# RMSNorm statistics of an encoder kernel: one full-precision product replaced by two on a high and a low part

## The chip, the cores and the metric

The kernel runs on one core of a Trainium2 chip. The metric is the time of one execution on the device in microseconds, the median of several runs. PE is the tensor engine, DVE the vector engine, ACT the scalar engine, POOL the GpSimd engine and SP the engine that issues most of the transfers; each runs its own instruction stream in order, and they meet only in semaphores.

## What is computed

A two-layer encoder trunk on 512 tokens of 1024 channels in float32. Layer 0 mixes tokens by 2-D neighbourhood attention, layer 1 by sliding-window attention; each is followed by a squared-ReLU MLP. An RMSNorm stands ahead of each of the four sub-layers and at the end.

```python
def rms_norm(x, g):
    xf = x.astype(jnp.float32)
    y = xf * lax.rsqrt(jnp.mean(xf * xf, axis=-1, keepdims=True) + EPS)
    return (y * g.astype(jnp.float32)).astype(x.dtype)

def reference(x, mix_norm, mlp_norm, final_norm, ...):
    for i in range(DEPTH):                      # DEPTH = 2
        h = rms_norm(x, mix_norm[i])
        if i % 2 == 0:
            x = x + neighbourhood_attention(h, ...)
        else:
            x = x + sliding_window_gqa(h, ...)
        h = rms_norm(x, mlp_norm[i])
        x = x + squared_relu_mlp(h, mlp_w_in[i], mlp_w_out[i])
    return rms_norm(x, final_norm)
```

## The kernel before

**Layout.** `x` is kept transposed in SBUF: channels on the 128 partitions in 8 tiles, k = 0 to 7, and 512 tokens along the free dimension. The weights stream in as 180 chunks of 8 blocks of 128x128, in two alternating buffers `w_raw`.

**Dense products.** Every value that enters a dense product is split into a high part (rounded to a shorter format, F32R, by a copy on ACT) and a low part (the value minus its high part, by DVE), and `product` issues three matmuls for each block: high by high, high by low, low by high (L370 to L372 in turn). A group is 8 such blocks and fills one of the two accumulators `acc`; it uses one chunk of weights. For chunk c ACT makes `w_hi` (L733) and DVE `w_lo` (L999); PE waits for `w_split` before the first block of a chunk and, from the third group on, for `acc_taken`, which says that DVE has read the accumulator.

**The norm.** There are five norms, n = 0 to 4. Norm 0 is at the start, 1 ahead of the first MLP, 2 ahead of the second attention, 3 ahead of the second MLP, and 4, the final one, is built differently (`last_squares`, `last_norm`, `last_statistics`). For each tile k, `prepare_x` on ACT makes `h_hi` (L743) and the square of `x` (L744), and `finish_x` on DVE makes `h_lo` (L1010) and adds the square to `sqsum` (L1016), which raises `h_split`. Ahead of norms 1 and 3 the tiles come from `output_projection`, ahead of norm 2 from the down loop of `mlp`. The dense product runs on the tiles not yet normalised. The scale is put on its result: the statistics product on PE (a matrix of ones by `sqsum`, so that each partition gets the sum over all channels, in full precision, L420), then `deviation` on ACT (square root, L757), `reciprocal_deviation` on DVE (L1021, 3.35 us), and `scale_tile` (L1027), which reads `acc`.

**Order around it.** The order on each engine is written out by hand. On PE, `part_after_norm` runs the first group behind a norm block by block as the tiles come, and puts the statistics ahead of the last block, k = 7. A second group follows; the third needs the third chunk of weights, whose `w_lo` stands on DVE behind the reciprocal and the first scaling. On ACT, `load_sqrt` is a tiny square root (128x1) that makes the table of that function come in ahead of the time it is needed. It stands at the end of `output_projection` and of each MLP half and ahead of the first `deviation`. Copies and squares run under any table; an exponential in attention brings in another one. `SPLIT_AFTER` says behind which tile which chunk is split.

Of the kernel before, what the change touches and what calls it, by code (L numbers as in the profile page):

```python
# [22 lines left out]
P = 128  # L23
# [75 lines left out]
def encoder(nc, xT, wstream, gains, rpb, sinks, rel_table, na_mask, onehot, out):  # L99
# [3 lines left out]
    with ExitStack() as ctx:  # L103
        def sb(name, shape, dt=F32):
            return ctx.enter_context(nc.sbuf_tensor(name, shape, dt))
# [24 lines left out]
        rstd = sb("rstd", [P, SEQ])  # L130
        scaled = sb("scaled", [P, 2, SEQ])
        ident, ones = sb("ident", [P, P]), sb("ones", [P, P])
        mask = sb("mask", [P, QT, WC])
# [37 lines left out]

        x_prepared, h_split, sq_cleared = sem("x_prepared"), sem("h_split"), sem("sq_cleared")
        stat_done, std_made, rstd_made = sem("stat_done"), sem("std_made"), sem("rstd_made")

# [192 lines left out]
        def _(pe):  # L367
# [49 lines left out]
            def statistics(n):  # L417

                pe.wait_ge(h_split, KT * (n + 1))
                nc.tensor.matmul(flat(misc_ps[:]), ones[:], sqsum[:], start=True, stop=True).then_inc(stat_done, 1)  # L420

            def part_after_norm(c, g, n):

                for k in ALL:
                    pe.wait_ge(h_split, KT * n + k + 1)
                    if k == KT - 1:
                        statistics(n)
                    part(c, g, h_tile, [k])

            def transpose_v(blocks):  # L430
# [259 lines left out]

            pe.wait_ge(filled, 1)
            pe.wait_ge(ident_made, 1)
            na_step(At(0), attend=False)
# [33 lines left out]
        def _(act):  # L727
# [23 lines left out]
            def load_sqrt():  # L751

                nc.scalar.activation(one[:, 0:1], ones[:, 0:1], ACT.Sqrt)

            def deviation(n):
# [60 lines left out]
            def na_step(m, dense=True, attend=True, before=True):  # L816
# [9 lines left out]
                if dense and m.a == 0:  # L826
                    load_sqrt()
                    deviation(0)
# [20 lines left out]
            def output_projection(ch, gr, norm):  # L849
                split_weights(At(ch + EARLY))  # L850
                for k in range(KT):
                    prepare_x(norm, At(k), lambda: act.wait_ge(acc_taken, gr + k + 1))
                    if k in SPLIT_AFTER:
                        split_weights(At(ch + SPLIT_AFTER[k]))
                load_sqrt()

            def last_squares():

                act.wait_ge(h_split, KT * NORMS - 2)
                for n, t in enumerate(half_tokens):  # L860
                    act.wait_ge(acc_taken, LAST_G + 1 + n)
                    nc.scalar.activation(last_square[:, t], x[:, KT - 1, t], ACT.Square).then_inc(x_prepared, 1)
                    if n == 0:
                        load_sqrt()
                    act.wait_ge(stat_done, NORMS + n)
                    nc.scalar.activation(rstd[:, t], last_stats[n], ACT.Sqrt, bias=eps[:], scale=1.0 / D
                                         ).then_inc(std_made, 1)

            def mlp(ch, gr, ti, sq, norm):
                for half in range(2):  # L870
# [17 lines left out]
                    def down(n, i):  # L888
# [7 lines left out]
                        if (c + 1).a < CHUNKS:  # L896
                            split_weights(c + 1)

                    with act.Fori(0, KT // 2 - 1) as i:
                        down(0, i)  # L900
                        down(1, i)
# [4 lines left out]
                    down(KT - 1, None)  # L906
                load_sqrt()

# [45 lines left out]
            act.wait_ge(filled, 2)  # L954
            nc.scalar.activation(one[:, 0:1], ones[:, 0:1], ACT.Square)
            split_weights(At(0))
            for k in range(KT):
                prepare_x(0, At(k), lambda: act.wait_ge(x_landed[k], 16))
                if k == 5:
                    split_weights(At(1))  # L960
            na_step(At(0), attend=False)
            na_step(At(1), before=False)
# [33 lines left out]
        def _(dve):  # L996
# [8 lines left out]
            def finish_x(n, k):  # L1005
# [8 lines left out]
                if tile.a >= 1:  # L1014
                    dve.wait_ge(h_split, tile.v)
                nc.vector.tensor_tensor(sqsum[:], sqsum[:], probs[:, SEQ * k.odd:SEQ * (k.odd + 1)],  # L1016
                                        ALU.add).then_inc(h_split, 1)

            def reciprocal_deviation(n):
# [137 lines left out]
            def output_projection(ch, gr, norm):  # L1157
# [8 lines left out]
                for k in range(KT):  # L1166
                    if k < EARLY - 1:
                        add(k + 1)
                    elif k >= EARLY:
                        add(k)  # L1170
                    finish_x(norm, At(k))
                    if k in SPLIT_AFTER:
                        split_weights(At(ch + SPLIT_AFTER[k]))

            def last_norm():
# [30 lines left out]
            def mlp(ch, gr, ti, norm):  # L1206
                for half in range(2):
# [28 lines left out]
                    if norm == 3 and half == 1:  # L1236
                        last_norm()
                        return
                    down(KT - 1, None)

            def sw_logits(p, n):
# [66 lines left out]
            nc.vector.memset(ones[:], 1.0).then_inc(filled, 1)  # L1308
            nc.vector.memset(eps[:], EPS).then_inc(filled, 1)
            clear_squares(0)  # L1310
            split_weights(At(0))
            dve.wait_ge(gain_landed, 16)
            for k in range(KT):
                finish_x(0, At(k))
                if k == 5:
                    split_weights(At(1))
            na_step(At(0), attend=False)
            dve.wait_ge(consts_landed, 16 * 2)
# [139 lines left out]
```

## Time and profile before

| | us |
|---|---|
| median of 3 runs | 1162.21 |
| lowest, highest | 1161.75, 1163.99 |
| the profiled execution, its time | 1161.89 |
| its span | 1160.2 |
| PE busy in it | 1136.2 (98%) |
| DVE, ACT busy | 640.2 (55%), 506.6 (44%) |

The span reaches from the first to the last instruction that the profiler recorded; the execution's time is 1.7 us longer. Times in the rows are microseconds from the start of the span. Matmuls overlap, so the distance from one start to the next says what one costs, and not its duration.

### The profile page before, as it was taken

To read this page: it belongs to the slowest core of one execution; us is meant where nothing else is said; L and a number is where in the kernel's file an instruction comes from. 1 tells how busy PE (TensorE), PEld (TensorE's weight loads), DVE (VectorE), ACT (ScalarE), POOL (GpSimd) and SP (SyncE) were. 2 spreads that over 40 slices of the span, in tenths; PEclk is the share of its full clock that TensorE was granted. 3 is DMA by queue.
4 is the path that set the end of the run, shared out by engine and by line. 5 is a ranking of instruction groups with operands and counts; after the bars stand their busy time and mean duration, and the time that the engine had idled before them with its cause. 6 is when DMAs were issued, how large, how long until landed. Compare 5 with 4: busy or idle time off the path is not lost.

```text
span 1160.2 us, 16677 instructions
## 1 busy us (share of the span) xinstructions
PE 1136.2 (98%) x5610; PEld 933.9 (80%) x5610; DVE 640.2 (55%) x1020; ACT 506.6 (44%) x907; POOL 136.7 (12%) x243
## 2 busy tenths in 40 slices
PE   6999999999999999999999999999999999999996
PEld 4788888878888888888887788787888888888886
DVE  7687888665443234443445787766544223544335
ACT  6677776654341124342233666644433112433221
POOL 4744532230000000000000222100000000000000
PEclk9999999999999999999999999999999999999999
DMA  7322231242322322322322122122332232232222
GB/s 212 108 84 74 68 104 57 82 124 92 107 91 91 108 91 91 108 90 91 108 83 81 57 58 64 51 73 78 103 104 96 90 106 93 90 105 95 90 90 91
DMA packets 36850, 106.73 MB, mean 92 GB/s; under 512 B 8224, under 2 KB 10544, under 8 KB 36816
## 3 DMA queue, kind: packets, MB, share of 16 engines
q1 hardware_dynamic: 31680, 98.98, 26.1%
q0 software_dynamic: 4992, 7.29, 2.8%
q8 instruction: 20, 0.33, 0.1%
q14 instruction: 14, 0.11, 0.0%
q10 hardware_dynamic: 144, 0.02, 0.0%
HBM read 102.92 MB, written 3.34 MB: 92 GB/s over the span
## 4 chain that ended last, share of the span: by engine, by line
PE 91%; DVE 3%; SPq 1%; issue 1%; ACT 1%; POOL 1%; DMA 0%; DVEq 0%; ACTq 0%; POOLq 0%
PE acc L370 27%; PE acc L371 26%; PE acc L372 26%; PE s_ps L442 3%; PE om_ps L476 2%; PE pt_ps L641 2%; PE om_ps L472 1%; PE om_ps L500 1%; PE pt_ps L463 1%; SPq L268 1%; PE om_ps L432 1%; POOL bias_pairs L298 1%; PE s_ps L370 1%; PE s_ps L372 1%; PE s_ps L371 1%
## 5 line engine op out<-in xcount | busy, mean ns | idle before, releaser
L733 ACT CAST w_hi<-w_raw 128x1024 fp32r<-128x1024 f32 x180 | 189.1, 1050 | 405.1 <-PE acc L372 401.3
L370 PE MATMUL acc<-h_hi,w_hi 128*128 128x512 f32 x800 | 324.0, 405 | 10.7 <-DVE sqsum L1016 10.2
L372 PE MATMUL acc<-h_hi,w_lo 128*128 128x512 f32 x800 | 313.2, 391 | 0.0
L371 PE MATMUL acc<-h_lo,w_hi 128*128 128x512 f32 x800 | 313.1, 391 | 0.0
L999 DVE TENSOR_TENSOR w_lo<-w_raw,w_hi 128x1024 fp32r<-128x1024 f32 x180 | 223.2, 1240 | 144.1 <-ACT w_hi L733 143.7
L370 PE MATMUL acc<-u_hi,w_hi 128*128 128x512 f32 (+1 forms) x624 | 241.4, 387 | 0.9 <-DVE w_lo L999 0.9
L372 PE MATMUL acc<-u_hi,w_lo 128*128 128x512 f32 (+1 forms) x624 | 239.5, 384 | 0.0
L371 PE MATMUL acc<-u_lo,w_hi 128*128 128x512 f32 (+1 forms) x624 | 239.4, 384 | 0.0
L370 PEld LDWEIGHTS acc<-h_hi,w_hi 128*128 128x128 f32 x800 | 151.0, 189 | 50.0 <-issue 14.1
L372 PEld LDWEIGHTS acc<-h_hi,w_lo 128*128 128x128 f32 x800 | 151.0, 189 | 32.4
L371 PEld LDWEIGHTS acc<-h_lo,w_hi 128*128 128x128 f32 x800 | 151.5, 189 | 29.0 <-issue 1.2
L1027 DVE SCALAR_TENSOR_TENSOR scaled<-acc,rstd 128x512 f32<-128x512 f32 x90 | 62.0, 688 | 143.3 <-PE acc L372 142.6
L370 PEld LDWEIGHTS acc<-u_hi,w_hi 128*128 128x128 f32 x624 | 117.2, 188 | 26.1 <-DVE w_lo L999 2.3
L372 PEld LDWEIGHTS acc<-u_hi,w_lo 128*128 128x128 f32 x624 | 117.3, 188 | 23.4
L371 PEld LDWEIGHTS acc<-u_lo,w_hi 128*128 128x128 f32 x624 | 117.3, 188 | 22.3
L320 POOL DMA_DIRECT2D bias_pairs<-t_shifted x64 | 32.2, 505 | 463.7 <-ACT esink L925 454.4
L777 ACT ACTIVATE probs<-probs,nmax 128x256 f32<-128x256 f32 (+1 forms) x128 | 67.9, 532 | 38.4 <-DVE nmax L1090 38.4
L1146 DVE TENSOR_TENSOR x_res<-acc,x_res 128x512 f32 (+1 forms) x39 | 26.9, 690 | 101.7 <-PE acc L372 101.7
L1037 DVE TENSOR_TENSOR u_lo<-scaled,u_hi 128x512 f32 (+1 forms) x80 | 58.5, 732 | 12.6 <-ACT u_hi L769 12.2
L310 POOL TENSOR_TENSOR bias_masked<-bias_pairs,mask 128x256 f32<-128x256 f32 x64 | 52.3, 857 | 75.1 <-DVE nmax L1090 73.2
L743 ACT ACTIVATE h_hi<-x_res,gain 128x512 fp32r<-128x512 f32 (+1 forms) x32 | 23.1, 722 | 71.9 <-DVE x_res L1146 62.9
L769 ACT CAST u_hi<-scaled 128x512 f32 (+1 forms) x80 | 49.8, 622 | 9.7 <-DVE scaled L1027 2.5
(107 smaller groups left out, 999.1 us busy)
## 6 DMA issues: line engine op xcount, KB each, us to landing
w_raw<-in_wstream SPq DMA_DIRECT2D x180, 512.0 KB, 3.3
bias_pairs<-rpb_shifted POOLq DMA_DIRECT2D x64, 48.0 KB, 2.9
bias_pairs<-t_shifted POOLq DMA_DIRECT2D x64, 48.0 KB, 2.2
x_res<-in_xT SPq DMA_DIRECT2D x8, 256.0 KB, 4.6
out_y<-x_res SPq DMA_DIRECT2D x16, 128.0 KB, 1.8
t_shifted<-vT POOLq DMA_DIRECT2D x16, 31.0 KB, 2.1
rpb_shifted<-rpb_pad POOLq DMA_DIRECT2D x8, 45.0 KB, 5.1
rpb_shifted<-rpb_pad SPq DMA_DIRECT2D x8, 45.0 KB, 7.6
```

Source lines behind the costliest of these rows:

```text
L310: ins = nc.gpsimd.tensor_tensor(bias_m[:, g, i, :, :].rearrange("p c r -> p r c"), rows[:, :, U0[j]:U0[j] + WC], mask[:, j:j + 1, :].to_br ...
L320: pool.dma_start(bias[QC * a:QC * (a + 1), pair.odd, :, :], t5_dram[:, heads, at:at + BAND]).then_inc(t5_bias_landed[pair.odd], 16)
L370: nc.tensor.matmul(dst, a[0], b[0], start=start, stop=False)
L371: nc.tensor.matmul(dst, a[0], b[1], start=False, stop=False)
L372: return nc.tensor.matmul(dst, a[1], b[0], start=False, stop=stop)
L442: ins = nc.tensor.matmul(dst(hh), a[s, queries[0], queries[1]], b[s, keys[0], keys[1]], start=start, stop=stop)
L733: nc.scalar.copy(w_hi[:, c.odd, :], w_raw[:, c.odd, :]).then_inc(w_hi_made, 1)
L769: nc.scalar.copy(dst, src).then_inc(tile_hi, 1)
L777: return nc.scalar.activation(src, src, ACT.Exp, bias=nmax[:, slot, i:i + 1], scale=-1.0, accum_out=rsum[:, slot, i:i + 1])
L999: nc.vector.tensor_tensor(w_lo[:, c.odd, :], w_raw[:, c.odd, :], f32(w_hi[:, c.odd, :]), ALU.subtract).then_inc(w_split, 1)
L1027: nc.vector.scalar_tensor_tensor(out=dst, in0=order(acc[g.odd][:]), scalar=factor, in1=order(rstd[:]), op0=op, op1=ALU.mult).then_inc(acc_ ...
L1037: nc.vector.tensor_tensor(order[0](dst), order[1](scaled[:, e.odd, :]), order[0](f32(hi)), ALU.subtract).then_inc(tile_split, 1)
```

## The change

The sum of squares is split like every other operand: ACT copies `sqsum` into `sq_hi`, rounded, and DVE subtracts to get `sq_lo`. The statistics of norms 0 to 3 become two products with a rounded matrix of ones (`ones_r`, made once at the start by DVE), and they stand behind block k = 7 of the first group instead of ahead of it. The final norm keeps its full-precision products. `load_sqrt` moves: to the very start in place of a tiny square, behind tile k = 3 (EARLY - 1) in `output_projection`, and ahead of the down loop in the second half of each MLP; the one in `last_squares` goes.

```diff
+        sq_hi, sq_lo = sb("sq_hi", [P, SEQ], F32R), sb("sq_lo", [P, SEQ], F32R)
+        ones_r = sb("ones_r", [P, P], F32R)
@@ PE
             def statistics(n):
 
-                pe.wait_ge(h_split, KT * (n + 1))
-                nc.tensor.matmul(flat(misc_ps[:]), ones[:], sqsum[:], start=True, stop=True).then_inc(stat_done, 1)
+                pe.wait_ge(sq_split, n + 1)
+                nc.tensor.matmul(flat(misc_ps[:]), ones_r[:], sq_hi[:], start=True, stop=False)
+                nc.tensor.matmul(flat(misc_ps[:]), ones_r[:], sq_lo[:], start=False, stop=True).then_inc(stat_done, 1)
 
             def part_after_norm(c, g, n):
 
                 for k in ALL:
                     pe.wait_ge(h_split, KT * n + k + 1)
-                    if k == KT - 1:
-                        statistics(n)
                     part(c, g, h_tile, [k])
+                statistics(n)
@@ ACT
+            def squares_high(n):
+
+                act.wait_ge(h_split, KT * (n + 1))
+                nc.scalar.copy(sq_hi[:], sqsum[:]).then_inc(sq_hi_made, 1)
@@ ACT, na_step
                 if dense and m.a == 0:
-                    load_sqrt()
                     deviation(0)
@@ ACT, output_projection
                     if k in SPLIT_AFTER:
                         split_weights(At(ch + SPLIT_AFTER[k]))
-                load_sqrt()
+                    if k == EARLY - 1:
+                        load_sqrt()
+                squares_high(norm)
@@ ACT, last_squares
-                    if n == 0:
-                        load_sqrt()
@@ ACT, mlp
+                    if half == 1:
+                        load_sqrt()
                     with act.Fori(0, KT // 2 - 1) as i:
                         down(0, i)
                         down(1, i)
...
                     down(KT - 1, None)
-                load_sqrt()
+                squares_high(norm + 1)
@@ ACT, start
-            nc.scalar.activation(one[:, 0:1], ones[:, 0:1], ACT.Square)
+            load_sqrt()
...
+            squares_high(0)
@@ DVE
+            def squares_low(n):
+
+                dve.wait_ge(sq_hi_made, n + 1)
+                nc.vector.tensor_tensor(sq_lo[:], sqsum[:], f32(sq_hi[:]), ALU.subtract).then_inc(sq_split, 1)
@@ DVE, end of output_projection
+                squares_low(norm)
@@ DVE, end of mlp
                     down(KT - 1, None)
+                    if half == 1:
+                        squares_low(norm + 1)
@@ DVE, start
+            dve.wait_ge(filled, 1)
+            nc.vector.tensor_copy(ones_r[:], ones[:]).then_inc(ones_rounded, 1)
...
+            squares_low(0)
```

In the listings that follow, the added lines have shifted the line numbers: the three matmuls of a block are L370 to L372 before and L373 to L375 after.

PE at norm 1, the end of the first group behind the norm (`acc<-h` are its blocks 6 and 7, `om_ps` is the bank that the statistics fill), before:

```order
L370 MATMUL acc<-h_hi,w_hi 128x512
L371 MATMUL acc<-h_lo,w_hi 128x512
L372 MATMUL acc<-h_hi,w_lo 128x512
L420 MATMUL om_ps<-sqsum,ones 128x512
L370 MATMUL acc<-h_hi,w_hi 128x512
L371 MATMUL acc<-h_lo,w_hi 128x512
L372 MATMUL acc<-h_hi,w_lo 128x512
```

And with the change:

```order
L373 MATMUL acc<-h_hi,w_hi 128x512
L374 MATMUL acc<-h_lo,w_hi 128x512
L375 MATMUL acc<-h_hi,w_lo 128x512
L373 MATMUL acc<-h_hi,w_hi 128x512
L374 MATMUL acc<-h_lo,w_hi 128x512
L375 MATMUL acc<-h_hi,w_lo 128x512
L423 MATMUL om_ps<-sq_hi,ones_r 128x512
L424 MATMUL om_ps<-sq_lo,ones_r 128x512
```

The statistics moved behind the three matmuls of block 7 and are two.

DVE at norm 1, from the last tile to the reciprocal, before:

```order
L1146 TENSOR_TENSOR x_res<-acc,x_res 128x512
L1010 SCALAR_TENSOR_TENSOR h_lo<-x_res,gain,h_hi 128x512
L1016 TENSOR_TENSOR sqsum<-sqsum,probs 128x512
L999 TENSOR_TENSOR w_lo<-w_raw,w_hi 128x1024
L1021 RECIPROCAL rstd<-rstd 128x512
```

And with the change:

```order
L1162 TENSOR_TENSOR x_res<-acc,x_res 128x512
L1021 SCALAR_TENSOR_TENSOR h_lo<-x_res,gain,h_hi 128x512
L1027 TENSOR_TENSOR sqsum<-sqsum,probs 128x512
L1010 TENSOR_TENSOR w_lo<-w_raw,w_hi 128x1024
L1033 TENSOR_TENSOR sq_lo<-sqsum,sq_hi 128x512
L1037 RECIPROCAL rstd<-rstd 128x512
```

The new subtraction stands behind the split of a weight chunk.

ACT ahead of norm 1, tiles 3 and 4 of `output_projection`, with the change:

```order
L737 CAST w_hi<-w_raw 128x1024
L747 ACTIVATE h_hi<-x_res,gain 128x512
L748 ACTIVATE probs<-x_res 128x512
L757 ACT_TABLE_LOAD
L757 ACTIVATE one<-ones 128x1
L747 ACTIVATE h_hi<-x_res,gain 128x512
L748 ACTIVATE probs<-x_res 128x512
```

The table load now stands between two tiles; before, it stood behind the last split of weights:

```order
L733 CAST w_hi<-w_raw 128x1024
L753 ACT_TABLE_LOAD
L753 ACTIVATE one<-ones 128x1
L757 ACTIVATE rstd<-om_ps,eps 128x512
L733 CAST w_hi<-w_raw 128x1024
```

In its old place comes the copy that makes `sq_hi`.

## Rows read from the trace of the kernel before

**Rows 1.** Page: engine's busy us, share, instructions; ACT's busy tenths in 40 slices.

```profile
PE 1136.2 (98%) x5610; PEld 933.9 (80%) x5610; DVE 640.2 (55%) x1020; ACT 506.6 (44%) x907; POOL 136.7 (12%) x243
...
ACT  6677776654341124342233666644433112433221
```

**Rows 2.** Waits of PE, whole span: us in total, times, longest.

```profile
PE acc L370 <- DVE sqsum L1016: 10.2, 4, 8.2
PE acc L370 <- DVE w_lo L999: 1.4, 4, 0.5
```

**Rows 3.** Timeline, PE, norms 1 and 3: start, duration, instruction, [idle before <-releaser].

```profile
256.80 0.40 PE L372 MATMUL acc<-h_hi,w_lo 128*128 128x512 f32 x1
257.03 1.02 PE L420 MATMUL om_ps<-sqsum,ones 128*128 128x512 f32 x2
...
258.13 0.40 PE L371 MATMUL acc<-h_lo,w_hi 128*128 128x512 f32 x1
...
263.81 0.39 PE L372 MATMUL acc<-h_hi,w_lo 128*128 128x512 f32 x1
...
264.78 0.39 PE L371 MATMUL acc<-h_lo,w_hi 128*128 128x512 f32 x1
...
803.07 1.02 PE L420 MATMUL om_ps<-sqsum,ones 128*128 128x512 f32 x2
```

**Rows 4.** Timeline, ACT, norm 1: the table load and the square root.

```profile
255.40 1.28 ACT L753 ACT_TABLE_LOAD   x1
256.69 0.20 ACT L753 ACTIVATE one<-ones 128x1 f32<-128x1 f32 x1
258.09 0.69 ACT L757 ACTIVATE rstd<-om_ps,eps 128x512 f32<-128x512 f32 x1 [1.20 <-PE om_ps L420]
```

**Rows 5.** Timeline, DVE, norm 1: last addition, splits before and behind the reciprocal.

```profile
255.14 0.69 DVE L1016 TENSOR_TENSOR sqsum<-sqsum,probs 128x512 f32<-128x512 f32 x1
255.74 1.22 DVE L999 TENSOR_TENSOR w_lo<-w_raw,w_hi 128x1024 fp32r<-128x1024 f32 x1
...
263.10 1.22 DVE L999 TENSOR_TENSOR w_lo<-w_raw,w_hi 128x1024 fp32r<-128x1024 f32 x1
```

**Rows 6.** Timeline, DVE and then PE, norm 2.

```profile
605.47 1.22 DVE L999 TENSOR_TENSOR w_lo<-w_raw,w_hi 128x1024 fp32r<-128x1024 f32 x1
...
612.54 1.22 DVE L999 TENSOR_TENSOR w_lo<-w_raw,w_hi 128x1024 fp32r<-128x1024 f32 x1
613.67 0.69 DVE L1037 TENSOR_TENSOR k_lo<-scaled,k_hi 128x512 fp32r<-128x512 f32 x1
...
606.76 1.02 PE L420 MATMUL om_ps<-sqsum,ones 128*128 128x512 f32 x2
...
614.14 0.40 PE L371 MATMUL acc<-h_lo,w_hi 128*128 128x512 f32 x1
```

**Rows 7.** Timeline, ACT around tile 3 ahead of norm 1, and PE behind it.

```profile
236.96 0.62 ACT L744 ACTIVATE probs<-x_res 128x512 f32<-128x512 f32 x1
239.60 0.72 ACT L743 ACTIVATE h_hi<-x_res,gain 128x512 fp32r<-128x512 f32 x1 [2.02 <-DVE x_res L1146]
...
246.69 0.50 PE L370 MATMUL acc<-u_hi,w_hi 128*128 128x512 f32 x1 [0.47 <-DVE w_lo L999]
```

**Rows 8.** Start: timeline of DVE, ACT, PE; windows with busy us by engine, PEclk, DMA.

```profile
17.57 0.68 DVE L1016 TENSOR_TENSOR sqsum<-sqsum,probs 128x512 f32<-128x512 f32 x1
...
19.83 0.69 ACT L757 ACTIVATE rstd<-om_ps,eps 128x512 f32<-128x512 f32 x1 [1.90 <-PE om_ps L420]
...
41.66 0.55 PE L463 MATMUL pt_ps<-ident,probs 128*128 128x128 f32 x3 [1.87 <-ACT probs L812]
...
18.90:22.20 3.30, 3.30 (x9) 2.23 (x8) 1.65 (x1) 1.73 (x2) 0.91 (x2) 0.53 0.71 176
43.00:46.00 3.00, 3.00 (x17) 2.36 (x17) 0.67 (x2) 2.85 (x4) 2.66 (x6) 0.50 0.33 70
```

**Rows 9.** Timeline, ACT, final norm: the first square root.

```profile
1146.23 0.47 ACT L866 ACTIVATE rstd<-om_ps,eps 128x256 f32<-128x256 f32 x1 [1.20 <-PE om_ps L592]
```

More of the change, by code:

```diff
@@ L172, in encoder @@
         x_prepared, h_split, sq_cleared = sem("x_prepared"), sem("h_split"), sem("sq_cleared")
+        ones_rounded, sq_hi_made, sq_split = sem("ones_rounded"), sem("sq_hi_made"), sem("sq_split")
         stat_done, std_made, rstd_made = sem("stat_done"), sem("std_made"), sem("rstd_made")
@@ L691, in _ @@
             pe.wait_ge(filled, 1)
+            pe.wait_ge(ones_rounded, 1)
             pe.wait_ge(ident_made, 1)
```

## The prediction

> **What bounds the kernel now.** I read the page's list of engines first: PE is busy for 98% of the span [rows 1], so a microsecond taken from PE is worth a microsecond only where nothing else ends last. The waits of PE come next, since they show such places [rows 2]. There are few. Most of the first is the start of the kernel; one of 1.9 us for ACT stands at 41.66 [rows 8]; four, none over 0.5 us, are for the low part of a weight chunk, `w_lo`, which DVE makes. Two of those four lie just behind the statistics that this change rewrites. So the question is what ends last there.
>
> The timeline of norm 1 (the norm ahead of the first MLP) shows it. PE reaches the statistics product at 257.03, one step of 0.23 behind the product at 256.80, so it waited for nothing [rows 3]. The second product of the last k block starts at 258.13; without the statistics it would have started one step of 0.23 after 257.03, at 257.26. The full-precision statistics cost PE 0.87. ACT starts the square root at 258.09, 1.06 after the statistics began [rows 4]. Then come DVE's reciprocal, the first scaling and, at 263.10, the subtraction that makes `w_lo` of the third chunk; it ends at 264.32 [rows 5]. PE's last product ahead of that chunk starts at 263.81 and its second product on it at 264.78 [rows 3], where two steps of 0.23 would give 264.27. PE stands still for 0.51, and the chain **statistics, square root, reciprocal, scaling, low part of the weights** ends last at norm 1. Norm 3 repeats it 546.04 later (the statistics at 803.07 [rows 3]) with the same durations. At norm 2 (ahead of the second attention) there is no loop entry between reciprocal and scaling; the low part ends at 613.76 and PE's second product starts at 614.14 [rows 6], about 0.15 late. All three norms are bound by this chain, norm 2 barely.
>
> **Statistics products.** Removed: 0.87 of PE per norm. Added: two products on rounded operands of the same shape, 128x512. The dense products on such operands are their nearest row, one step of 0.23 each, so 0.46. PE's own work falls by 0.41 per norm. Only where PE is last is that a gain.
>
> **Order.** The statistics now stand behind the last k block, not ahead of it. That block is three steps, 0.68. At norm 1 the first statistics product can then start at 257.03 + 0.68 = 257.71 at the earliest. The second starts 0.23 later, lasts 0.39 like each dense product, and the square root follows its end by 0.04 (before: the second half of the old product ended at 258.05). Square root at 257.71 + 0.23 + 0.39 + 0.04 = 258.37, against 258.09: the chain starts **0.28 later**, although its product is cheaper.
>
> **High and low part.** PE now waits for `sq_lo`. After the last addition to `sqsum`, which ends at 255.83, ACT copies the sum (0.62, the price of ACT's square of the same shape [rows 7]), to about 256.5. ACT is free for it at 255.38, since the table load at 255.40 is gone [rows 4]. DVE first makes `w_lo` (from 255.74) and can follow 1.13 after that start, which is the distance between the `w_lo` row at 612.54 and the subtraction at 613.67 [rows 6]. So `sq_lo` starts at 256.87, later than the copy ends, and takes 0.69 as the subtraction at 613.67 does: it ends at 257.56. From a released `w_lo` to a moving PE the trace takes 0.23 (264.32 to 264.55, one step ahead of 264.78). PE's first statistics product moves at 257.79, 0.08 behind the 257.71 that its order allows. Norm 2, from 605.47: 606.60 + 0.69 + 0.23 = 607.52 against 606.76 + 0.68 = 607.44, again 0.08. Norm 3 the same. Behind PE's waiting product are the eight k blocks of the second group; they have slack, since the third group waits for the chain anyway.
>
> The chain is thus 0.28 + 0.08 = **0.36 late** at norms 1 and 3. PE's third group starts when it says so; the 0.41 that PE saved becomes a longer wait. At norm 2 `w_lo` ends at 613.76 + 0.36 = 614.12; by norm 1's distance of 0.46 the second product starts at 614.58, by norm 2's own of 0.38 at 614.50, against 614.14: 0.36 to 0.44, and I take 0.40. Sum: 0.36 + 0.40 + 0.36 = **1.12 us longer**. Bounds: if `sq_lo` costs no delay, 3 x 0.28 = 0.84; if release lags by another 0.1 each time, 1.4. Behind these places the PE rows show no wait that could swallow it.
>
> **Table load.** At norms 1 and 3 the load (1.28) and its tiny activation (0.20) move from behind the last tile to behind the fourth, k = 3. There ACT ends a square at 237.58 and starts the next tile at 239.60, idle for 2.02 [rows 7]; 1.48 fits, with 0.5 over. At its old place the load cost nothing either: ACT idled 1.20 ahead of the square root [rows 4]. Inside the first and the last MLP half the tiny activation (0.20) now comes ahead of the down loop, where ACT is busy for a quarter to a half of the time (around the middle and in the last third of the slices [rows 1]). At norm 0 the load becomes the first load of the kernel, in place of another of the same price. Sum: 0. The cover is thin at k = 3, because ACT and DVE hand each tile to one another there and PE waits for the outcome (0.47 at 246.69 [rows 7]): every microsecond over 0.5 would reach PE, twice. The load's row is followed by the activation at once (255.40 + 1.28 = 256.68, then 256.69), so I expect none. The Trainium skill, page "ScalarE: Activation LUTs", section "What ACT_TABLE_LOAD costs", speaks against this: it counts 1283 ns and some 1380 ns of drain for each switch, 2.66 us. By that, 0.84 would stick out at each of two places, 1.7 in all. Its 1283 ns agree with the row; the drain does not show in it.
>
> **Norm 0.** From the end of the last addition (17.57 + 0.68 = 18.25) to the square root the kernel takes 1.58 now [rows 8]. It would take 0.04 + 0.62 + 0.04 + 0.68, then 0.23 to PE, and at the halved clock, which the rows grant from 18.9 to 22.2 (0.53 of full, 1.2 GHz for nearly all of it), 0.43 + 0.63 + 0.04: 2.71, so 1.1 more. The third group would start about when it does now, for PE is ahead by the cheaper product. Whatever is left of it, at most 1.1, meets the wait of 1.87 at 41.66, whose releaser hangs on the attention bias that POOL loads and masks and not on the norm. Price 0, between 0 and 0.5. The copy `ones_r` runs while DVE waits for the first weights. **Final norm:** only a tiny activation goes, and ACT idles 1.20 ahead of that square root [rows 9]: 0.
>
> **Sum against the profiled execution.** Its span is 1160.20 and its time 1161.89, so 1163.0 after. It lies 0.32 below the median of the three runs, 1162.21; the same step from the median gives **1163.3**.
>
> **Rivals.**
> (a) The saving reaches the end. If the chain had slack, PE's 0.41 would come off three times: 1162.2 - 1.2 = 1161.0. For it: 98% busy. Against it: PE's waits on `w_lo` at norms 1 and 3. Chance 0.10.
> (b) The clock falls, which ends slower. PE's standstill at norm 1 grows to 0.51 + 0.41 + 0.36 - 0.08 = 1.20. The rows show the granted clock halved after the wait of 1.87 at 41.66 [rows 8] and around 18.9, behind the start's waits; after 0.47 at 246.69 no matmul was slower. 1.20 lies between. A stretch like that at 18.9 is 3.3 us at half speed and costs about 1.7. It decides from one fall on: 1165.0 with one, 1168.4 with three. Chance 0.08.
> (c) The table load holds ACT longer than its row. Taken as two loads and the activation, 2.77, it would stick out by 0.75 at two places: 1164.8. By the skill's page, as above, 1165.0. Chance 0.04.
> (d) The change doesn't do what it says: products on rounded operands cost as much as the full-precision one. Then PE's second statistics product starts 0.64 later and ends later by 0.2 to 0.5, so about 1 us more at each norm, 1166. The dense rows speak against it. Chance 0.02.
> (e) Forecast, 1163.3: chance 0.76. Its own range is 1162.4 to 1164.5, from the bounds above and the scatter of the three runs (2.2 us from lowest to highest).
>
> **Range and chances.** 1161.6 to 1165.2 holds nearly all of (e), (c) and one fall of (b); it leaves out most of (a), two or three falls and (d). A measurement of this kernel can tell about 0.2%, 2.3 us, from no change. Faster than 1159.9 needs (a) and luck: 0.02. Slower than 1164.5 is (b), (c), (d) and the upper tail of (e): 0.14. The same: 0.84.
>
> **What would show it.** In the profile after, PE's wait for `w_lo` behind norms 1 and 3 should be 1.0 to 1.2, and one of about 0.8 should appear at norm 2; the square root of norm 1 should start 1.3 to 1.45 after the end of the seventh k block, where it is 1.06 now. ACT's fifth tile should still be released by DVE's addition. The granted clock should be full behind all three. I am wrong if PE's waits there shrink, if the clock falls, or if the wait at 246.69 grows.

## The result and the profile after

| | before | after |
|---|---|---|
| median, runs taken in turn on the same chip | 1163.22 us (1161.66 to 1165.56, 22 runs) | 1164.36 us (1163.42 to 1166.13, 22 runs) |
| ratio, 95% interval | | 1.0013 (1.0007 to 1.0019) |
| span of the profiled execution | 1160.2 | 1162.7 |

The medians differ by 1.14 us; the ratio, taken between runs that stand beside one another, is 0.13% or 1.5 us. It is a small loss, with an interval that excludes no change, but inside the 0.2% that the prediction calls the same. The forecast was 1163.3, 1.1 over the 1162.21 that it started from.

PE's busy time fell and the span grew. The page of the kernel after, with the engines as in [rows 1]:

```profile
PE 1134.8 (98%) x5610; PEld 933.2 (80%) x5610; DVE 642.4 (55%) x1025; ACT 507.5 (44%) x909; POOL 136.2 (12%) x243
```

PE is 1.4 less busy, DVE 2.2 more. PE's waits, as in [rows 2]:

```profile
PE acc L373 <- DVE sqsum L1027: 10.7, 5, 8.2
PE pt_ps L466 <- ACT probs L821: 3.5, 1, 3.5
PE acc L373 <- DVE w_lo L1010: 3.4, 5, 0.9
```

The waits for `w_lo` went from 1.4 to 3.4 us and from four to five. The timeline of PE shows where they are: norm 1 from its block 7 on (compare [rows 3]), then the first matmuls of the third group at norms 2 and 3.

```profile
258.65 0.39 PE L373 MATMUL acc<-h_hi,w_hi 128*128 128x512 f32 x1
...
259.33 0.41 PE L423 MATMUL om_ps<-sq_hi,ones_r 128*128 128x512 f32 x1
259.58 0.40 PE L424 MATMUL om_ps<-sq_lo,ones_r 128*128 128x512 f32 x1
259.81 0.39 PE L373 MATMUL acc<-h_hi,w_hi 128*128 128x512 f32 x1
...
266.37 0.49 PE L373 MATMUL acc<-h_hi,w_hi 128*128 128x512 f32 x1 [0.93 <-DVE w_lo L1010]
266.70 0.39 PE L374 MATMUL acc<-h_lo,w_hi 128*128 128x512 f32 x1
...
615.99 0.50 PE L373 MATMUL acc<-h_hi,w_hi 128*128 128x512 f32 x1 [0.57 <-DVE w_lo L1010]
616.33 0.40 PE L374 MATMUL acc<-h_lo,w_hi 128*128 128x512 f32 x1
...
812.96 0.49 PE L373 MATMUL acc<-h_hi,w_hi 128*128 128x512 f32 x1 [0.92 <-DVE w_lo L1010]
813.29 0.40 PE L374 MATMUL acc<-h_lo,w_hi 128*128 128x512 f32 x1
```

Read it in this way. The two products cost 0.25 + 0.23 = 0.48 of PE (259.33 to 259.81), where the old one cost 0.87, so PE got its gain. But PE came to block 7 at 258.65, and ACT's square root starts 1.36 behind that, at 260.01 (the rows of ACT follow). Before, PE came to the same place at 257.03 and the root followed 1.06 behind. The chain (statistics, square root, reciprocal, scaling, low part of the weights) is 0.30 late and the third group with it: its second product starts 8.05 behind 258.65, where it was 7.75 behind 257.03. The rows of ACT and DVE for the same stretch (compare [rows 4, 5]):

```profile
257.49 0.62 ACT L762 CAST sq_hi<-sqsum 128x512 fp32r<-128x512 f32 x1 [0.47 <-DVE sqsum L1027]
260.01 0.69 ACT L766 ACTIVATE rstd<-om_ps,eps 128x512 f32<-128x512 f32 x1 [1.90 <-PE om_ps L424]
...
257.37 1.22 DVE L1010 TENSOR_TENSOR w_lo<-w_raw,w_hi 128x1024 fp32r<-128x1024 f32 x1
258.50 0.69 DVE L1033 TENSOR_TENSOR sq_lo<-sqsum,sq_hi 128x512 fp32r<-128x512 f32 x1
260.73 3.35 DVE L1037 RECIPROCAL rstd<-rstd 128x512 f32<-128x512 f32 x1 [1.54 <-ACT rstd L766]
```

**Where the 2.5 us between the two profiles went.** A span mixes places. I take the same four marks in both traces: the second product of the third group behind norms 1, 2 and 3, and the end. Where a kernel below has "distances" of +0.68 and +0.64, these are its last two columns of this table against the kernel before.

| kernel | to norm 1, shift against before | norm 1 to norm 2 | norm 2 to norm 3 |
|---|---|---|---|
| before | 0 (264.78) | 349.36 | 196.67 |
| after | +1.92 (266.70) | +0.27 | +0.29 |

Behind norm 3 all kernels of this study take 349.3 to 349.4. The +1.92 are 1.62 that PE is late already at block 7 of norm 1, and 0.30 of norm 1's chain. So the norms give 0.30 + 0.27 + 0.29 = **0.86 us**, and 1.6 come from the start of the kernel, which varies from run to run by as much (below). The traces show the place. PE's last product ahead of the transposes of the first attention starts 0.03 apart, and the transposes start 1.65 apart, behind a wait of 1.87 before and of 3.49 after. PE, the kernel before and then the kernel after:

```profile
39.39 0.40 PE L372 MATMUL acc<-h_hi,w_lo 128*128 128x512 f32 x1
41.66 1.09 PE L463 MATMUL pt_ps<-ident,probs 128*128 128x128 f32 x8 [1.87 <-ACT probs L812]
...
39.42 0.40 PE L375 MATMUL acc<-h_hi,w_lo 128*128 128x512 f32 x1
43.31 1.97 PE L466 MATMUL pt_ps<-ident,probs 128*128 128x128 f32 x8 [3.49 <-ACT probs L821]
```

Over 22 runs most of that scatter averages out.

### The profile page after: what moved, and what is told of

Its sections match the earlier page's. It is cut to its first block, busy times and chain, and to the rows that moved or that the text cites. A ratio compares the mean times of both kernels' runs of the same rounds, so it can differ in the third digit from the quotient of the medians.

```text
span 1162.7 us, 16680 instructions
## 1 busy us (share of the span) xinstructions
PE 1134.8 (98%) x5610; PEld 933.2 (80%) x5610; DVE 642.4 (55%) x1025; ACT 507.5 (44%) x909; POOL 136.2 (12%) x243
## 4 chain that ended last, share of the span: by engine, by line
PE 90%; DVE 4%; issue 1%; ACT 1%; POOL 1%; SPq 1%; DMA 1%; DVEq 0%; ACTq 0%; POOLq 0%
PE acc L373 26%; PE acc L375 25%; PE acc L374 25%; PE s_ps L445 3%; PE om_ps L479 2%; PE pt_ps L644 2%; PE om_ps L475 1%; PE om_ps L503 1%; PE pt_ps L466 1%; DVE w_lo L1010 1%; SPq L271 1%; DVE rstd L1037 1%; PE om_ps L435 1%; POOL bias_pairs L301 1%; PE s_ps L373 1%
## 5 line engine op out<-in xcount | busy, mean ns | idle before, releaser
L373 PE MATMUL acc<-h_hi,w_hi 128*128 128x512 f32 x800 | 321.8, 402 | 13.1 <-DVE sqsum L1027 10.7
L375 PE MATMUL acc<-h_hi,w_lo 128*128 128x512 f32 x800 | 313.0, 391 | 0.0
L373 PE MATMUL acc<-u_hi,w_hi 128*128 128x512 f32 (+1 forms) x624 | 241.4, 387 | 0.9 <-DVE w_lo L1010 0.9
L375 PE MATMUL acc<-u_hi,w_lo 128*128 128x512 f32 (+1 forms) x624 | 239.5, 384 | 0.0
L373 PEld LDWEIGHTS acc<-h_hi,w_hi 128*128 128x128 f32 x800 | 150.8, 188 | 52.4 <-issue 14.4
L375 PEld LDWEIGHTS acc<-h_hi,w_lo 128*128 128x128 f32 x800 | 150.8, 188 | 32.3
L373 PEld LDWEIGHTS acc<-u_hi,w_hi 128*128 128x128 f32 x624 | 117.2, 188 | 26.2 <-DVE w_lo L1010 2.6
L375 PEld LDWEIGHTS acc<-u_hi,w_lo 128*128 128x128 f32 x624 | 117.2, 188 | 23.3
L786 ACT ACTIVATE probs<-probs,nmax 128x256 f32<-128x256 f32 (+1 forms) x128 | 67.9, 533 | 39.4 <-DVE nmax L1106 39.4
```

Of the source, the lines that this page charges most:

```text
L373: nc.tensor.matmul(dst, a[0], b[0], start=start, stop=False)
L375: return nc.tensor.matmul(dst, a[1], b[0], start=False, stop=stop)
L786: return nc.scalar.activation(src, src, ACT.Exp, bias=nmax[:, slot, i:i + 1], scale=-1.0, accum_out=rsum[:, slot, i:i + 1])
```

## The experiments

The ratio of each is against the kernel before, run in turn with it on the same chip. The first four ran beside 35 runs of the kernel before (median 1162.85 us), the other four beside 29 (1163.24).

### The order alone

The kernel before, with the full-precision statistics moved behind block 7.

```diff
                 for k in ALL:
                     pe.wait_ge(h_split, KT * n + k + 1)
-                    if k == KT - 1:
-                        statistics(n)
                     part(c, g, h_tile, [k])
+                statistics(n)
```

> The kernel before with one edit: the full-precision statistics product stands behind block k = 7 of the first group, not ahead of it. Nothing is split, no table load moves. Chain theory (the chain from the statistics to the low part of the third weight chunk ends last at norms 1 to 3): the square root comes one block, 0.68 us, later at each norm, so the time grows by 3 x 0.68 = 2.0 us; PE's wait for w_lo at norm 1 grows from 0.5 to 1.2 of standstill. PE-bound theory (98% busy, order is free): 0.

Measured: 1164.64 us (1164.31 to 1166.63), ratio 1.0020 (1.0011 to 1.0029). PE at norm 1, from block 7 on, and the root on ACT:

```profile
257.67 0.39 PE L370 MATMUL acc<-h_hi,w_hi 128*128 128x512 f32 x1
...
258.36 1.02 PE L420 MATMUL om_ps<-sqsum,ones 128*128 128x512 f32 x2
...
265.77 0.49 PE L370 MATMUL acc<-h_hi,w_hi 128*128 128x512 f32 x1 [0.94 <-DVE w_lo L998]
...
259.42 0.69 ACT L756 ACTIVATE rstd<-om_ps,eps 128x512 f32<-128x512 f32 x1 [1.88 <-PE om_ps L420]
```

The root comes 1.75 behind 257.67, not 1.06: the order costs 0.69, three steps. (A step is the 0.23 from the start of one dense product to the start of the next.) The distances grow by 0.68 and 0.64. The place of the statistics costs 0.64 to 0.69 at each norm, about 2.0 in all, as expected. In the changed kernel the cheaper product pays for part of it.

### The table load alone

The kernel before, with `load_sqrt` in its new places.

```diff
                 if dense and m.a == 0:
-                    load_sqrt()
                     deviation(0)
@@ output_projection
+                    if k == EARLY - 1:
+                        load_sqrt()
-                load_sqrt()
@@ last_squares
-                    if n == 0:
-                        load_sqrt()
@@ mlp
+                    if half == 1:
+                        load_sqrt()
                     with act.Fori(0, KT // 2 - 1) as i:
...
-                load_sqrt()
@@ start
-            nc.scalar.activation(one[:, 0:1], ones[:, 0:1], ACT.Square)
+            load_sqrt()
```

> The kernel before with only the table loads moved as in the change. Theory: the load fits into the 2.02 us that ACT idles behind tile 3, so 0 (within 0.3), and PE's wait at 246.69 stays 0.47. Rival (the load holds ACT for longer than its row): about 0.75 to 0.84 at each of two places, 1.5 to 1.7 us slower, and that wait of PE grows by as much. At the start nothing should move either: the first block row of PE and the last addition of DVE where they were within 0.1.

Measured: 1163.37 us (1161.06 to 1165.08), ratio 1.0005 (0.9997 to 1.0014). ACT ahead of norm 1 (compare [rows 7]):

```profile
238.59 1.28 ACT L753 ACT_TABLE_LOAD   x1
239.88 0.20 ACT L753 ACTIVATE one<-ones 128x1 f32<-128x1 f32 x1
240.59 0.72 ACT L743 ACTIVATE h_hi<-x_res,gain 128x512 fp32r<-128x512 f32 x1 [0.51 <-DVE x_res L1145]
```

The next tile still waits for DVE's addition, with 0.51 over. The Trainium skill, page "ScalarE: Activation LUTs", section "What ACT_TABLE_LOAD costs", gives 1283 ns for the load, which this row shows, and some 1380 ns of drain, which the rows do not show: the activation starts 1.29 behind the load's start. PE's `w_lo` waits are 1.4, four times, as before, and the distances between the norms are 349.35 and 196.63, as before. The moved loads cost nothing between norm 1 and norm 3. The +0.5 of the median can't be told from zero.

### The two products, ahead of block 7

The changed kernel, with its statistics back in the old place.

```diff
                     pe.wait_ge(h_split, KT * n + k + 1)
+                    if k == KT - 1:
+                        statistics(n)
                     part(c, g, h_tile, [k])
-                statistics(n)
```

> The changed kernel with one edit: the two statistics products stand ahead of block k = 7 again, as the single one did before the change. If sq_lo (ACT's copy, DVE's split of the weights, DVE's subtraction) is as late as the order of PE, the square root starts where it does in the changed kernel within 0.1, PE stands still some 0.7 ahead of the products and some 0.7 less behind the second group, and the time is that of the changed kernel, 0.9 to 1.1 over before. If only the order costs, the chain starts 0.68 earlier, and the time is about 1.1 below before (0.3 - 0.68 = -0.4 at each norm).

Measured: 1165.09 us (1162.21 to 1166.34), ratio 1.0016 (1.0007 to 1.0025). The saving doesn't come back: PE now stands in front of the statistics and waits for `sq_lo`.

```profile
256.19 0.39 PE L375 MATMUL acc<-h_hi,w_lo 128*128 128x512 f32 x1
257.10 0.47 PE L423 MATMUL om_ps<-sq_hi,ones_r 128*128 128x512 f32 x1 [0.52 <-DVE sq_lo L1034]
257.41 0.40 PE L424 MATMUL om_ps<-sq_lo,ones_r 128*128 128x512 f32 x1
```

PE is there one step behind 256.19, at 256.42, and the root starts at 257.84, 1.42 behind, 0.36 more than before. The distances grow by 0.33 and 0.38. That is about 1.1 for three norms, as expected; the interval of the ratio, 0.8 to 2.9 us, holds it. So the new place behind block 7 is not a fault by itself: it hides the making of `sq_lo`, and either place costs about 0.3 to 0.36. What binds is that **the split is ready only 1.7 us behind the last addition** (256.77 + 0.68 to 258.50 + 0.69 in the rows of after), where the full-precision product needed the addition alone.

### Norm 0 as before

The changed kernel, with norm 0's statistics in full precision ahead of block 7 and its table load at its old place.

```diff
-                pe.wait_ge(sq_split, n + 1)
+                if n == 0:
+                    pe.wait_ge(h_split, KT)
+                    nc.tensor.matmul(flat(misc_ps[:]), ones[:], sqsum[:], start=True, stop=True).then_inc(stat_done, 1)
+                    return
+                pe.wait_ge(sq_split, n)
...
                     pe.wait_ge(h_split, KT * n + k + 1)
+                    if n == 0 and k == KT - 1:
+                        statistics(n)
                     part(c, g, h_tile, [k])
-                statistics(n)
+                if n > 0:
+                    statistics(n)
@@ ACT, start
-            load_sqrt()
+            nc.scalar.activation(one[:, 0:1], ones[:, 0:1], ACT.Square)
...
-            squares_high(0)
@@ DVE, squares_low
-                dve.wait_ge(sq_hi_made, n + 1)
+                dve.wait_ge(sq_hi_made, n)
@@ DVE, start
-            squares_low(0)
```

> The changed kernel with norm 0 as before the change (one full-precision product ahead of block 7, a table load ahead of its square root); norms 1 to 3 as changed. If the start takes no part, as predicted, the time is that of the changed kernel within 0.3, with about 0.3 us at each of norms 1 to 3, 0.9 over before, and the difference of 1.65 us at 41 us between the two first profiles is scatter of the transfers. If the change at norm 0 delays the attention bias, this kernel is 0.2 to 1.6 us faster than the changed one.

Measured: 1164.06 us (1162.27 to 1165.94), ratio 1.0012 (1.0003 to 1.0021), the changed kernel's own 1.0013. The distances are +0.24 and +0.28, as after. Norm 0 costs nothing that shows, although its root is 1.19 later: in the trace after it starts at 21.02 (19.83 in [rows 8]). The medians alone would not show less than about 1 us. The traces before and after show more: at 39.4, some 18 us behind the root of norm 0, PE is 0.03 apart (the rows in the section on the result).

```profile
21.02 0.69 ACT L766 ACTIVATE rstd<-om_ps,eps 128x512 f32<-128x512 f32 x1 [2.04 <-PE om_ps L424]
```

### Statistics earlier, not cheaper

If the chain ends last and PE has work to spare ahead of it, the old full-precision product should pay by coming earlier. The kernel before, with the statistics ahead of block 6 at norms 1 to 3. PE waits there for the last tile's sum as before, and blocks 6 and 7 then run behind the statistics.

```diff
                     pe.wait_ge(h_split, KT * n + k + 1)
-                    if k == KT - 1:
+                    if k == (KT - 1 if n == 0 else KT - 2):
                         statistics(n)
```

> The kernel before with one edit: at norms 1 to 3 the full-precision statistics product stands ahead of block k = 6, one block earlier (norm 0 as it was). Its cost on PE stays 0.87 us. The sum it needs is there at 255.83 in the trace of before, and PE reaches block 6 at 256.35. Chain theory: the chain starts 0.68 earlier at each norm and stops ending last, PE's standstill behind the second group (0.51, 0.15, 0.51) goes, so 1.2 us faster than before; the distance between PE's third groups of norms 1 and 2 shrinks by 0.15, of norms 2 and 3 by 0.5. PE-bound theory (only what PE works counts): 0.

Measured: 1161.55 us (1159.85 to 1165.13), ratio 0.9985 (0.9976 to 0.9994): faster by 1.7. The wait list of PE holds only the two waits for `w_lo` ahead of norms 1 and 3 (one is the 0.47 at 246.69 in [rows 7]); those behind the norms are gone.

```profile
PE acc L370 <- DVE w_lo L999: 0.9, 2, 0.5
```

The distances are −0.21 and −0.55. At norm 2 only the small standstill was there to take; at norm 3 all of it, 0.5. Norm 1 gives 0.48: from the last product ahead of the wait at 246.69 (245.83; here 248.80) to the second product of the third group (264.78; here 267.27) PE takes 18.95 before and 18.47 here. So the traces show 1.2 of the 1.7, as much as expected; the interval of the ratio, 0.7 to 2.8 us, holds both, and what the rest is stays open.

### Both places mended

The changed kernel, with the statistics ahead of block 7 and DVE's `sq_lo` ahead of its last split of weights.

```diff
@@ PE, part_after_norm
+                    if k == KT - 1:
+                        statistics(n)
                     part(c, g, h_tile, [k])
-                statistics(n)
@@ DVE, output_projection
                     finish_x(norm, At(k))
+                    if k == KT - 1:
+                        squares_low(norm)
                     if k in SPLIT_AFTER:
                         split_weights(At(ch + SPLIT_AFTER[k]))
-                squares_low(norm)
@@ DVE, mlp
                             finish_x(norm + 1, m)
+                            if i is None and n == KT - 1:
+                                squares_low(norm + 1)
...
-                    if half == 1:
-                        squares_low(norm + 1)
```

> The changed kernel with two edits: the statistics ahead of block 7, and DVE's subtraction sq_lo ahead of its last split of weights, not behind it. Chain theory: both things that hold the chain (the order on PE and sq_lo) are eased, PE waits some 0.3 ahead of the products, and the square root comes 1.16 after PE has reached block 7, against 1.06 before and 1.36 changed: 0.1 per norm over before, 0.3 in all, and 0.6 under the changed kernel. If the loss of the changed kernel lay elsewhere (table load, the two extra instructions, clock), this kernel would be as slow as it, 0.9 over before.

Measured: 1162.03 us (1161.25 to 1163.79), ratio 0.9994 (0.9985 to 1.0003). DVE, then PE, at norm 1:

```profile
255.45 0.68 DVE L1028 TENSOR_TENSOR sqsum<-sqsum,probs 128x512 f32<-128x512 f32 x1
256.82 0.69 DVE L1034 TENSOR_TENSOR sq_lo<-sqsum,sq_hi 128x512 fp32r<-128x512 f32 x1 [0.69 <-ACT sq_hi L763]
...
257.11 0.39 PE L375 MATMUL acc<-h_hi,w_lo 128*128 128x512 f32 x1
257.66 0.47 PE L423 MATMUL om_ps<-sq_hi,ones_r 128*128 128x512 f32 x1 [0.16 <-DVE sq_lo L1034]
```

PE is at the statistics at 257.34 and the root, at 258.40, starts 1.06 behind: exactly the kernel before. The distances are −0.02 and −0.02. I had expected +0.3; the price of ACT's copy, DVE's subtraction and two hand-overs is met by the cheaper product to within what the trace shows. The split is then worth nothing that the traces show, but costs nothing. The changed kernel's 0.86 is gone, although the moved table loads and the two added instructions are still there.

### The high part alone

The changed kernel without the low part in the statistics of norms 0 to 3 (so they are less exact; this is left out of the computation), with its one product ahead of block 7.

```diff
-                pe.wait_ge(sq_split, n + 1)
-                nc.tensor.matmul(flat(misc_ps[:]), ones_r[:], sq_hi[:], start=True, stop=False)
-                nc.tensor.matmul(flat(misc_ps[:]), ones_r[:], sq_lo[:], start=False, stop=True).then_inc(stat_done, 1)
+                pe.wait_ge(sq_hi_made, n + 1)
+                nc.tensor.matmul(flat(misc_ps[:]), ones_r[:], sq_hi[:], start=True, stop=True).then_inc(stat_done, 1)
@@ PE, part_after_norm
+                    if k == KT - 1:
+                        statistics(n)
                     part(c, g, h_tile, [k])
-                statistics(n)
@@ DVE
-                squares_low(norm)
...
-                    if half == 1:
-                        squares_low(norm + 1)
...
-            squares_low(0)
```

> The changed kernel with the low part left out of the statistics of norms 0 to 3 (one product on sq_hi, no subtraction, so that the sum is that of the rounded squares), ahead of block 7. It shows what the cheap product is worth when nothing holds it up. Chain theory: the copy is done before PE reaches block 7, the square root starts 0.43 after that instead of 1.06, so the chain is 0.63 shorter and is still the last to end; norms 1 and 3 gain 0.63 each, norm 2 about 0.5 to 0.63: 1.8 us faster than before. If the copy on ACT is late, up to 0.3 less at each.

Measured: 1161.12 us (1159.38 to 1163.0), ratio 0.9985 (0.9976 to 0.9994). The distances are −0.65 and −0.61. ACT makes the copy in time:

```profile
255.75 0.62 ACT L762 CAST sq_hi<-sqsum 128x512 fp32r<-128x512 f32 x1 [0.48 <-DVE sqsum L1027]
257.36 0.69 ACT L766 ACTIVATE rstd<-om_ps,eps 128x512 f32<-128x512 f32 x1 [0.98 <-PE om_ps L423]
```

PE's one product starts at 256.93 without a wait, and the root 0.43 behind it, 0.63 sooner than the 1.06 of before. That is what a cheaper product is worth when nothing is put ahead of it. The low part, with its subtraction and second product, takes all of it back.

### Earlier statistics and an earlier split of weights

The kernel before with the statistics ahead of block 6, and the seventh chunk of weights of the output projection split one tile sooner, for the two waits that were left.

```diff
-SPLIT_AFTER = {0: 5, 2: 6, 5: 7, 6: 8, 7: 9}
+SPLIT_AFTER = {0: 5, 2: 6, 4: 7, 6: 8, 7: 9}
...
-                    if k == KT - 1:
+                    if k == (KT - 1 if n == 0 else KT - 2):
                         statistics(n)
```

> A try at a faster version: early_full, and in both output projections chunk 7 is split behind tile 4 instead of tile 5, so that PE's other wait for w_lo (0.47 at 246.69, some 0.7 of standstill, and its twin 546 us later) goes. Expected: 1.2 + 2 x 0.7 = 2.6 us faster than before. If DVE's earlier split holds back the next addition and with it the tiles of the norm (ACT and DVE hand each tile to one another there), the second part is lost and PE waits behind the norm's first blocks instead: 1.2 faster or less.

Measured: 1159.40 us (1158.81 to 1161.25, 7 runs), ratio 0.9968 (0.9957 to 0.9979): the fastest of the study, and ahead of both kernels. PE's list of waits from its top:

```profile
PE acc L370 <- DVE sqsum L1016: 9.9, 3, 8.2
PE pt_ps L463 <- ACT probs L812: 5.5, 1, 5.5
PE pt_ps L592 <- ACT probs L862: 1.0, 1, 1.0
PE om_ps L420 <- DVE sqsum L1016: 0.4, 1, 0.4
```

No wait for `w_lo` is left. Norm 1 to norm 2 takes 0.20 less and norm 2 to norm 3 1.34 less, of which 0.55 are the earlier statistics, as in the run with the earlier statistics alone. The rest, 0.79, is the wait of 0.46 that went at norm 3's projection and what such a wait costs beside its idle time: at norm 1 the list shows 0.26 where the starts of the products stand 0.51 too far apart [rows 3], 0.25 more, which makes 0.71. With norm 1 as norm 3, the traces account for about 2.9 of the 3.7 us; the interval of the ratio is 2.4 to 5.0.

## Why the prediction was right

**What bounds the kernel.** Right, and the reading that carried the case. Three edits that lengthen the chain lose, whatever they do to PE's busy time (the changed kernel, order alone, two products ahead of block 7), and two that shorten it win (statistics earlier, high part alone). The high part alone wins by what the chain lost, 0.6 at each norm. The earlier statistics take three steps, 0.68, off the chain and win only the standstill that was there, 0.5 or less: behind that the chain no longer ends last. PE was 98% busy in all of them.

**Price of the products.** 0.46 forecast, 0.48 shown. Rival (d) is out.

**Order.** 0.28 forecast. The chain is 0.30 late; the 0.02 are the two products' distance of 0.25 where I took a step of 0.23. The run of the order alone shows the 0.68 in it.

**`sq_lo`.** This term, 0.08 each time, was over-sized: it measured none. DVE did as forecast (258.50 is 1.13 behind 257.37), so `sq_lo` ended at 259.19, but I let 0.23 pass from its end to a moving PE. I had reckoned that back from the second matmul after a wait, to a first one at 264.55. The trace before has the first one at 264.45, 0.13 behind the end of `w_lo` at 264.32, and the second 0.33 behind the first, not one step:

```profile
264.45 0.49 PE L370 MATMUL acc<-h_hi,w_hi 128*128 128x512 f32 x1 [0.26 <-DVE w_lo L999]
```

Behind `sq_lo` the first one starts 0.15 behind the end: in the run with two products ahead of block 7, 256.27 + 0.68 to 257.10, and in the mended one 257.51 to 257.66. By that PE could go at 259.34 here, where its order let it go at 259.33. The release came just in time, with nothing to spare; that is also why the wait shows up in full once the statistics stand ahead of block 7.

**Norm 2.** Forecast was 0.40, between 0.36 and 0.44; shown is 0.27. The difference is the same 0.08, and the choice between two distances from `w_lo` to PE. From the root to the second product norm 2 takes 6.33 after (610.00 to 616.33) and 6.32 before (607.82 to 614.14), so norm 2's own distance held.

**Sum.** 1.12 was forecast and 0.86 is in the trace. The interval of the ratio is 0.8 to 2.2 us and holds both. Whether anything beyond the norms' 0.86 is real stays open: the start scatters by more. That the medians differ by 1.14, next to the forecast, is therefore in part luck. The time itself came out 1.1 over the forecast's 1163.3, because the median of three runs that it started from was 1.0 under the median of 22.

**Table load and norm 0.** For both 0 was forecast. ACT's fifth tile was still released by DVE, with the 0.5 over that was forecast:

```profile
239.22 1.28 ACT L757 ACT_TABLE_LOAD   x1
240.52 0.20 ACT L757 ACTIVATE one<-ones 128x1 f32<-128x1 f32 x1
241.23 0.72 ACT L747 ACTIVATE h_hi<-x_res,gain 128x512 fp32r<-128x512 f32 x1 [0.51 <-DVE x_res L1162]
```

PE's wait behind it is 0.47 as before, now at 248.32. Rival (c) is out, in both its forms. At norm 0 the root was forecast 1.1 late against the last addition. It came at 21.02, 2.69 behind that addition's end (17.65 + 0.68), where it took 1.58 before: 1.1. The run with norm 0 as before shows no gain from undoing it.

**Clock.** Rival (b) did not happen. Windows of the trace after, behind norms 1, 2 and 3 (length, busy us of PE, PEld, DVE, ACT, POOL, granted clock, share and GB/s of the transfers):

```profile
250.00:270.00 20.00, 19.07 (x84) 15.32 (x84) 14.52 (x15) 9.00 (x13) 0.00 (x0) 1.00 0.28 98
600.00:620.00 20.00, 19.43 (x85) 15.61 (x84) 12.25 (x12) 6.11 (x8) 0.00 (x0) 1.00 0.28 95
800.00:815.00 15.00, 14.08 (x62) 11.21 (x62) 10.80 (x11) 7.16 (x10) 0.00 (x0) 1.00 0.27 93
```

The clock stayed full, 2.4 GHz, behind waits of 0.93, 0.57 and 0.92.

**Where "what would show it" was off.** The waits at norms 1 and 3 were forecast as 1.0 to 1.2 and the list shows 0.93 and 0.92; 0.8 at norm 2, and it shows 0.57. I had counted standstill from start to start, from the second product back to the last product ahead of the wait, less two steps; the list counts from the modelled end of one matmul to the start of the next. By my own count the three are 1.19 (265.05 to 266.70), 0.84 and 1.18, where 1.20, 0.8 and 1.20 were forecast. By the list the waits of before at these places are smaller in the same measure: 0.26 at norm 1, where I read 0.51. The growth, 0.93 − 0.26 = 0.67, is 0.39 that PE saved (0.87 − 0.48) plus 0.30, to 0.02.

## What to carry to other kernels

- A cheaper instruction pays only if its result comes sooner. Before making an operation cheaper, follow its result to the next thing that another engine waits for, and ask what the cheaper form needs first (here a copy, a subtraction and two hand-overs).
- Where a chain through other engines ends last and the bound engine has independent work in front, put the chain's first step ahead of that work. That one condition in the code brought 1.7 us, and with one weight split moved, 3.7 (1.2 and 2.9 of it can be read in the traces); the rewrite of the arithmetic lost 1.1 to 1.5.
- To compare two traces of 1160 us for an effect of 0.3, measure distances between the same marks on both sides of the effect. Spans carry the scatter of the start: the profiled execution with the earlier statistics has a span of 1161.9, more than the 1160.2 before, though its kernel is the faster one.

## What the runs showed beside

**The start scatters by more than the effect.** The transposes of the first attention start on PE between 41.55 and 43.93 in the ten traces, and wait from 0.8 to 5.5 us there. Kernels that are alike up to that point differ as well: 41.66 before, 43.88 with the statistics earlier at norms 1 to 3. Behind the wait stand POOL's 16 loads of the attention bias and the masking after them. The kernel after (its transposes start at 43.31, shown above), then the one with the two products ahead of block 7:

```profile
22.65 8.03 POOL L301 DMA_DIRECT2D bias_pairs<-rpb_shifted  x16 [11.53 <-DMA rpb_shifted<-rpb_pad]
35.40 5.59 POOL L313 TENSOR_TENSOR bias_masked<-bias_pairs,mask 128x256 f32<-128x256 f32 x8 [3.14 <-DMA sink<-in_sinks]
```

```profile
21.13 8.00 POOL L301 DMA_DIRECT2D bias_pairs<-rpb_shifted  x16 [9.88 <-DMA rpb_shifted<-rpb_pad]
32.21 6.62 POOL L313 TENSOR_TENSOR bias_masked<-bias_pairs,mask 128x256 f32<-128x256 f32 x8 [1.51 <-DMA sink<-in_sinks]
41.55 1.09 PE L467 MATMUL pt_ps<-ident,probs 128*128 128x128 f32 x8 [0.77 <-ACT probs L822]
```

The masking starts 3.2 apart; by the profile it waits for a transfer each time. Why that transfer lands sooner or later was not tried.

**The granted clock goes with it.** From 41.5 to 49.0 the kernel after was granted 0.77 of full and that with the two products ahead of block 7 the full clock:

```profile
41.50:49.00 7.50, 5.69 (x33) 4.86 (x34) 3.02 (x12) 5.86 (x12) 6.17 (x11) 0.77 0.23 56
```

```profile
41.50:49.00 7.50, 7.35 (x45) 5.97 (x46) 5.76 (x14) 6.54 (x16) 6.69 (x12) 1.00 0.20 46
```

In the ten traces it is 1.00 where PE's wait ahead of the transposes was 0.77, 0.83 and 1.13, and 0.77 or less where it was 1.87 or more. The three with the full clock are also those whose rounded statistics of norm 0 stand ahead of block 7. Nothing here tells whether that is the cause or chance; the medians show no gain that would need it.
